# ScalarE's order of reading out a bank and splitting a weight block, in three kinds of steps

## The reference

```python
def mamba2_mixer(h, norm_w, in_w, conv_w, conv_b, ...):
    u = rms_norm(h, norm_w)
    zxbcdt = u @ in_w                       # the scan projections
    z, xbc, dt = jnp.split(zxbcdt, [D_INNER, D_INNER + CONV_CH], axis=-1)
    xbc = jax.nn.silu(conv(xbc, conv_w) + conv_b)      # causal, width 4
    ...
    y = ssd_chunked(xs, dt, a, bm, cm) + d_skip * xs   # chunks of 128 tokens
    y = y.reshape(b, s, D_INNER) * jax.nn.silu(z)
    yg = y.reshape(b, s, SSM_GROUPS, D_INNER // SSM_GROUPS)
    yg = yg * lax.rsqrt(jnp.mean(yg * yg, axis=-1, keepdims=True) + EPS)
    return (yg.reshape(b, s, D_INNER) * gnorm_w) @ out_w
# attention: q, gate = split(u @ attn_in_w); out = (swa(rope(q), k, v) * silu(gate)) @ attn_out_w
# embedding: h + act(rms_norm(h) @ ple_gate_w) * (p @ ple_proj_w)    (the p product: "embedding projection")
```

## Time and profile before

| | us |
|---|---|
| median of three runs | 1388.23 (1386.51 to 1390.5) |
| the profiled execution, its own time | 1387.61 |
| its span on the core | 1385.1 |
| TensorE busy | 1350.1 (97%) |
| VectorE busy | 831.0 (60%) |
| ScalarE busy | 677.9 (49%) |
| GpSimd busy | 525.6 (38%) |

### The profile page before, as it was taken

The page is one execution under the profiler, slowest core; times in us unless marked ns, Lnnn a source line. Parts: engine busy times, 40 slices in busy tenths (PEclk is TensorE's granted clock), DMA queues, the critical chain, the costliest instruction groups (busy, mean ns, idle before and its releaser), DMA issues.

```text
span 1385.1 us, 17824 instructions
## 1 busy us (share of the span) xinstructions
PE 1350.1 (97%) x6628; PEld 1062.1 (77%) x6628; DVE 831.0 (60%) x1417; ACT 677.9 (49%) x1130; POOL 525.6 (38%) x259
## 2 busy tenths in 40 slices
PE   9989999999999999999999999999999999999997
PEld 6867778777688878767888887766667888888886
DVE  6775554757567744785677323477755645544666
ACT  7664635636466533784565312355545332232463
POOL 3553544636220134466000344136433655555200
PEclk9999999999999999999999999999999999999999
DMA  5221222222123232211233232130012232332331
GB/s 196 94 74 47 92 70 83 77 72 77 65 97 102 77 92 93 63 44 55 99 91 122 97 135 87 37 116 16 17 46 76 94 104 91 97 101 92 122 107 61
DMA packets 33796, 116.93 MB, mean 84 GB/s; under 512 B 4140, under 2 KB 4652, under 8 KB 33456
## 3 DMA queue, kind: packets, MB, share of 16 engines
q1 hardware_dynamic: 32408, 111.62, 25.1%
q10 hardware_dynamic: 1304, 4.19, 0.8%
HBM read 113.70 MB, written 2.10 MB: 84 GB/s over the span
## 4 chain that ended last, share of the span: by engine, by line
PE 88%; DVE 5%; ACT 3%; issue 2%; DMA 1%; POOL 1%; ACTq 0%; DVEq 0%
PE bank L1306 85%; PE bank L1762 1%; PE bank L1604 1%; DMA h<-in_xT 0%; ACT wsh L864 0%; DVE arena L1957 0%; POOL arena L773 0%; DVE arena L2037 0%; PE bank L1480 0%; PE bank L1515 0%; DMA ring<-in_wstream 0%; DVE wsl L1843 0%; DVE arena L2329 0%; DVE ssacc L1838 0%; DVE arena L2243 0%
## 5 line engine op out<-in xcount | busy, mean ns | idle before, releaser
L710 POOL TENSOR_TENSOR wsl<-ring,wsh 128x1024 fp32r<-128x1024 f32 x143 | 348.8, 2440 | 543.6 <-ACT wsh L864 543.4
L864 ACT ACTIVATE wsh<-ring 128x1024 fp32r<-128x1024 f32 x196 | 207.2, 1058 | 452.8 <-PE bank L1306 429.9
L1306 PE MATMUL bank<-parts1h,wsh 128*128 128x512 f32 (+1 forms) x736 | 292.8, 398 | 6.1 <-POOL wsl L710 2.2
L1306 PE MATMUL bank<-parts1h,wsl 128*128 128x512 f32 (+1 forms) x736 | 285.6, 388 | 0.0
L1306 PE MATMUL bank<-parts1l,wsh 128*128 128x512 f32 (+1 forms) x736 | 285.6, 388 | 0.0
L1306 PE MATMUL bank<-parts0h,wsh 128*128 128x512 f32 x696 | 277.8, 399 | 3.8 <-issue 1.3
L1306 PE MATMUL bank<-parts0h,wsl 128*128 128x512 f32 x696 | 271.3, 390 | 0.0
L1306 PE MATMUL bank<-parts0l,wsh 128*128 128x512 f32 x696 | 271.1, 390 | 0.0
L1306 PEld LDWEIGHTS bank<-parts1h,wsh 128*128 128x128 f32 x736 | 138.6, 188 | 43.1 <-issue 9.7
L1306 PEld LDWEIGHTS bank<-parts0h,wsh 128*128 128x128 f32 x696 | 130.7, 188 | 40.9 <-issue 10.8
L1306 PEld LDWEIGHTS bank<-parts1l,wsh 128*128 128x128 f32 x736 | 138.8, 189 | 28.8 <-issue 2.2
(11 more groups left out here) (322 smaller groups left out, 1802.7 us busy)
## 6 DMA issues: line engine op xcount, KB each, us to landing
ring<-in_wstream SPq DMA_DIRECT2D x204, 512.0 KB, 3.5
arena<-in_alibi ACTq DMA_DIRECT2D x2, 1024.0 KB, 5.1
outT<-arena SPq DMA_DIRECT2D x8, 256.0 KB, 2.8
h<-in_xT SPq DMA_DIRECT2D x4, 256.0 KB, 6.3
h<-in_xT ACTq DMA_DIRECT2D x4, 256.0 KB, 5.8
ring<-in_wstream SPq DMA_DIRECT2D x2, 256.0 KB, 4.5
arena<-in_frow ACTq DMA_DIRECT2D x1, 512.0 KB, 3.4
arena<-in_cmpb ACTq DMA_DIRECT2D x1, 496.0 KB
```

The costliest lines, as they stand in the source:

```text
L710: return nc.gpsimd.tensor_tensor(dst, src, hi.bitcast(F32), ALU.subtract)
L864: nc.scalar.activation(wsh[n % NSET][:, :], src, ACT.Copy).then_inc(*done("high", ("high", L)))
L1306: return nc.tensor.matmul(*args, **kw)
```

## The change

ScalarE's loop over the splits of a step becomes a function, `weight_high`. For a step of the kinds proj, gate and pp it is called at the end of ScalarE's part of the step, after the readout (and, in a projection, after the opened SiLU), and not at its head; for every other kind it stays at the head. The other engines' programs are the same.

```diff
--- before.py
+++ after.py
@@ -848,20 +848,26 @@
                 k, a = step[0], step[1:]
                 if k == "ple" and a[1]:
                     square(2 * a[0] + 2 if a[0] < 2 else 7, a[1] - 1)
-                for b, n in splits_at(step):
-
-                    L = BLKNO[b]
-                    act.wait_ge(*at("loaded", L))
-                    src = ring[:, L % NSLOT, :]
-                    if n is None:
-
-                        act.wait_ge(*at("mm", *[("proj", 3, 9), ("gate", KD - 1), ("upv", FT - 1)][b[1]]))
-                        nc.scalar.activation(hnh[:, 6:8, :], src.rearrange("p (a b) -> p a b", a=2), ACT.Copy)\
-                            .then_inc(*done("high", ("high", L)))
-                    else:
-                        if n >= NSET:
-                            act.wait_ge(*at("set_free", n - NSET))
-                        nc.scalar.activation(wsh[n % NSET][:, :], src, ACT.Copy).then_inc(*done("high", ("high", L)))
+                def weight_high():
+
+                    for b, n in splits_at(step):
+
+                        L = BLKNO[b]
+                        act.wait_ge(*at("loaded", L))
+                        src = ring[:, L % NSLOT, :]
+                        if n is None:
+
+                            act.wait_ge(*at("mm", *[("proj", 3, 9), ("gate", KD - 1), ("upv", FT - 1)][b[1]]))
+                            nc.scalar.activation(hnh[:, 6:8, :], src.rearrange("p (a b) -> p a b", a=2), ACT.Copy)\
+                                .then_inc(*done("high", ("high", L)))
+                        else:
+                            if n >= NSET:
+                                act.wait_ge(*at("set_free", n - NSET))
+                            nc.scalar.activation(wsh[n % NSET][:, :], src, ACT.Copy).then_inc(*done("high", ("high", L)))
+
+                late = k in ("proj", "gate", "pp")
+                if not late:
+                    weight_high()
                 if k == "fw":
                     n, half = a
                     c = slice(SEQ * half, SEQ * half + SEQ)
@@ -1278,6 +1284,8 @@
 
                         act.wait_ge(*at("mm", "dn", m // 4 - 2, KD - 1))
                     nc.scalar.activation(xgh[:, m % 8, :], fsl[m % 2], ACT.Copy).then_inc(*done("ffhi", ("ffhi", m)))
+                if late:
+                    weight_high()
 
         @block.tensor
         def _(pe):
```

## The result

The changed kernel takes 1394.74 us (median of five runs, 1393.54 to 1395.73) against 1388.61 for the kernel before in the runs beside it: a ratio of 1.0048, 95% interval 1.0034 to 1.0062, so 4.7 to 8.6 us slower. The forecast was 1395.2. The profiled execution took 1393.54 with a span of 1391.5, 6.4 longer than before. In the experiments a difference in us is worked out from the ratio to the kernel before in the runs beside it (1.0010 is 1.4 us).

A forecast was written before the change was run, and what follows sets the result against it. TensorE, busy 1350.1 of 1385.1 us, was taken as the bound, so only its waits count. Terms 2.6 - 1.9 + 1.1 + 1.85 + 1.2 - 1.05 + 3.3, with small ones, gave +7.0: median 1395.2 us, range +4.2 to +10.

The forecast's parts named there:

- first projections, two remainders late: 40 to 76 us: TensorE waits for two remainders delayed behind readout, table load and SiLU; +2.6 us, bounds 1.5 to 3.4.
- group 0's scan, bank waits: 76 to 104 us: VectorE's taps start 0.95 us earlier, so three TensorE bank waits shrink; -1.9 us, bounds 0 to 2.6.
- end of group 1, of group 2: Before the seventh projection two readouts delay a remainder without slack; in group 2 the gating is held too: +1.1, +1.85 us.
- other small waits and collisions of the groups: Two small bank waits take off 0.3 us, smaller collisions in the last group give some 0.2 back.
- embedding projections, three places: Last embedding projections: VectorE's low halves come later, 0.4 us lost three times; +1.2 us, bounds 0 to 1.5.
- bank before the second query block: TensorE's 1.02 us wait for the bank freed by the fourth gate's readout goes; -1.05 us with the overlap.
- rotary chain and eighth gate: Three remainders hold the last rotary chain, ending at 578.5 instead of 574.38; the eighth gate starts 3.3 us late.
- Rival 3: The remainder delays the state's decay on GpSimd and TensorE feels it in four groups: +11 us, 1399; chance 0.08.
- Rival 1: Earlier taps carry everything along and the collisions don't happen: -0.4 us, near 1387.8; chance 0.26.
- Rival 2: Only the banks count, as SiLU's table load runs ahead in the first projections: -4.4 us, 1383.8; chance 0.06.
- The prediction's rule: A VectorE operation with two SBUF inputs and a GpSimd operation block each other whole; a remainder costs a chain its length.

The follow-up runs named there:

- e6: Kernel before, but in each group's first six projections ScalarE reads the bank out, then splits, then opens the SiLU: 1382.65 us, ratio 0.9958.
- e8: Changed kernel, but GpSimd's remainder at gates 5, 6 and 7 covers 256 of 1024 columns: 1389.64 us, ratio 1.0010.
- e7: Kernel before, with readout, split, SiLU in each group's first six projections, and the first four gates split late: 1381.72 us, ratio 0.9956.
- e2: Kernel before, with the split late in the eight gates alone: 1391.55 us, ratio 1.0026.
- e5: Kernel before, with the split late in the first four gates alone: 1386.37 us, ratio 0.9990.
- e9: Kernel before, with the split late in the seventh gate alone: 1385.98 us, ratio 0.9993.
- e4: Changed kernel, but four of 49 splits go first again (projections 2 and 4 of group 0, the seventh of groups 1 and 2): 1389.34 us, ratio 1.0010.
- e10: Kernel before, with the split late in the fifth and sixth gates alone: 1392.44 us, ratio 1.0042.
- e1: Kernel before, with the split late in the 35 projections alone: 1390.54 us, ratio 1.0017.
- e3: Kernel before, with the split late in the embedding projections alone: 1390.39 us, ratio 1.0011.

## Why the prediction was right, point by point

The direction was right for the reasons given: each of the places named is there, with its sign. That the total came out to 0.5 us (1395.2 against 1394.74) is partly luck: the steps that were priced came out smaller, 5.3 against 7.0, and terms that were not priced, the clock above all, brought the two profiled executions to 6.4 apart. The steps, by the balance of the two profiled executions, in us:

| step | predicted | measured |
|---|---|---|
| first projections, two remainders late | +2.6 | +1.46 +1.00 |
| group 0's scan, bank waits | -1.9 | -0.49 -0.93 -0.60 -0.46 |
| end of group 1, of group 2 | +1.1, +1.85 | +0.80, +1.51 |
| other small waits and collisions of the groups | -0.1 | 0.0 |
| embedding projections, three places | +1.2 | +0.43 +0.41 +0.41 |
| bank before the second query block | -1.05 | -1.00 |
| rotary chain and eighth gate | +3.3 | -0.88 +3.61 |
| clock behind the eighth gate | none | +2.6 |
| behind 1070 us | none | -2.0 |

**First projections.** As worked out, for the reason given: ScalarE's timeline of the changed kernel has the readout, a table load, a wait for the taps, the SiLU, and only then the split.

```profile
49.03 1.28 ACT L843 ACT_TABLE_LOAD   x1
50.73 0.63 ACT L843 ACTIVATE arena<-arena 128x512 f32<-128x512 f32 x1 [0.41 <-DVE arena L1965]
51.27 1.04 ACT L866 ACTIVATE wsh<-ring 128x1024 fp32r<-128x1024 f32 x1
```

e6 shows that the SiLU with its table load was all of it: with the split ahead of it TensorE waits for neither remainder.

**Group 0's scan.** The sum was too small by 0.6. The first wait was to gain 0.2, since the later remainder meets VectorE's preparation. It does, and holds it for 0.90 us, more than the 0.75 assumed. But the preparation itself starts 0.91 earlier, with the earlier taps in front of it, and VectorE had 0.38 of idle time before the next taps; this the prediction left out, and 0.49 was gained. In e6 the remainder comes 0.5 sooner, holds the preparation for 0.38 only, and the whole 0.92 comes. The sum also left out the wait of 0.39 at 101.29: it goes and gives 0.60, while of the 0.90 behind it only 0.46 goes.

**Ends of groups 1 and 2.** Right in place, 0.3 too high each; in group 2 the gating L2065, three operations, took 3.43 us and not 1.89, as the remainder ran until 227.0. The two readouts in front of the split cost 1.0 in both, nearly as priced. Too high was what stands ahead of them: less the balance, ScalarE's squares came 0.54 later in group 2, where 0.7 was taken, and 0.18 earlier in group 1, where nothing was taken. The tenth of a us for handovers doesn't show: in group 2 TensorE starts 0.15 us after the remainder's end, and 0.14 before.

**The groups' small terms** were the weak step. The sum of 0.0 hides four: small waits gone at the second chunk of group 1's scan (-0.77 together), then +0.72 there; +0.78 in group 2, and -0.74 behind it. The +0.72 is the mechanism of the prediction at a place where it wasn't looked for: VectorE's operation L1988, 1.21 us before (L1980 there, at 165.92), is held by a moved remainder in the changed kernel.

```profile
166.03 2.16 DVE L1988 TENSOR_TENSOR parts1h<-parts1l,con 64x1024 fp32r<-64x1024 f32 x1
...
164.72 2.40 POOL L710 TENSOR_TENSOR wsl<-ring,wsh 128x1024 fp32r<-128x1024 f32 x1 [3.56 <-ACT wsh L866]
```

The +0.78 comes of the order on GpSimd: the moved remainder, held itself to 3.37 us, stands in front of GpSimd's scan work L756 of the same step, which then holds VectorE's next operation. It came once, at 266.

```profile
263.49 3.37 POOL L710 TENSOR_TENSOR wsl<-ring,wsh 128x1024 fp32r<-128x1024 f32 x1 [3.91 <-ACT wsh L866]
266.81 1.05 POOL L756 TENSOR_TENSOR arena<-arena,cums 128x512 f32<-128x512 f32 x1
...
266.88 2.06 DVE L2030 SCALAR_TENSOR_TENSOR arena<-arena 128x1024 f32<-128x1024 f32 x1 [2.27 <-ACT arena L1021]
```

Before, that operation began at 264.36 and took 1.23; with the balance of 2.58 it begins on time (the wait for ScalarE is no loss), and takes 0.83 longer.

Rival 3's wait is there too. VectorE's sum of the states stands waiting for the decay L764 at seven places, 10.5 us together and 2.5 at most; before it was four places, 3.1 us and 0.9 at most. VectorE's timeline of the changed kernel at one of them:

```profile
105.65 0.69 DVE L2052 TENSOR_TENSOR arena<-arena,bank 128x512 f32<-128x512 f32 x1 [2.48 <-POOL arena L764]
```

But the balance doesn't rise behind any of the seven: TensorE doesn't feel it, as the prediction said against this rival.

**Gates.** The prediction asked for three operations above 2.3 us: they are 2.61, 2.63 and 2.71. It put the chain's end at 578.5; it is 580.0, less the balance of 2.12 that it came in with, 577.9. The eighth gate is 2.7 late, net, not 3.3: the wait of 0.69 for the seventh gate's readout goes (-0.88), and the wait behind the chain costs 3.61. Rival 1's condition, a chain that ends by 575.1, is what e8 brings about by the short remainder, and with it the eighth gate's wait goes. Rival 2 (only the banks count) fails in the first projections: the table load does run ahead of the wait, but the split stands behind the SiLU, and TensorE waits for the remainder. Its -4.4 lies between what the kernels get that keep the bank gains alone: by the balance -4.1 (e6) and -5.1 (e7, up to the second query block).

**What was missed** is the clock. It added 2.6 us in the changed kernel's profile. Behind 1070 us 2.0 fell away: 1.5 at 1074, where the clock fell in the kernel before and not in the changed one, and 0.5 at 1305, where kernels with no split moved after the gates (e2, e5, e9) gain 0.4 to 0.7 as well. So neither is a later stage giving time back, and the total came out right with unpriced terms against each other. This is the account of one execution of each kernel; how much of it the other executions share is not shown. The priced steps sum to 5.3 by the balance, against 7.0 predicted; group 0's scan, the ends of the groups and the eighth gate make 0.6 of the difference each.

## What to carry to other kernels

Moving an instruction to the end of its step delays everything that the step holds, also what only waits for others (here an opened SiLU and its table load); putting it behind the one instruction that mattered kept the gain and lost none of the time. Price such a move by slack, place by place: four of 49 moved splits carried 5 us, two others nearly 6, and most nothing. Here a GpSimd operation of 2.4 to 2.8 us that landed in a gapless VectorE chain cost it 2.0 to 2.2, and two of them made the chain long enough for the next one to fall inside.

## What was not expected of the hardware

**The clock falls after some waits, and not each time.** After the eighth gate's wait of 3.64 us (changed kernel, e2, e4) or 2.68 us (e10) matmuls of 0.39 us took 0.63 for a while, in all four traces; right behind the eighth gate of the eight without that wait they didn't. It took 2.6 us in the changed kernel and 1.5 to 1.6 in the other three. But the feed-forward part has a wait of 2.21 us that every kernel has alike, and there it goes both ways. Kernel before, then the changed one (TensorE):

```profile
1074.02 0.77 PE L1306 MATMUL bank<-parts1h,wsh 128*128 128x512 f32 x1 [2.21 <-POOL wsl L710]
1074.58 0.63 PE L1306 MATMUL bank<-parts1l,wsh 128*128 128x512 f32 x1
```

```profile
1082.01 0.47 PE L1314 MATMUL bank<-parts1h,wsh 128*128 128x512 f32 x1 [2.21 <-POOL wsl L710]
1082.32 0.39 PE L1314 MATMUL bank<-parts1l,wsh 128*128 128x512 f32 x1
```

The granted clock from 1065 to 1090 us was 0.93 in six of the twelve traces and 1.00 in six; it costs 1.5 us when it falls. It goes both ways at shorter waits too: behind one of 1.6 to 1.8 us for ScalarE, 11 to 14 us after the eighth gate's start, the clock fell in five of the twelve (e1, e2, e3, e5, e8; 1.2 to 1.3 us each), and behind the bank wait of 1.96 us near 81, which six traces have, in two (e3, e10; 1.6 us). What decides it at the shorter waits stays open. For a balance of two single traces it means that a us or two at such a place is no effect of an edit.

**VectorE is held in one-input operations too.** The scan's preparation L2009, a TENSOR_SCALAR of 64x512 with its input in SBUF, took 0.47 us before (L2001 there) and 1.37 in the changed kernel, where a remainder ran from 74.98 to 77.38 (in e6 0.85, where one ran until 74.09 and the operation ended at 74.37):

```profile
76.30 1.37 DVE L2009 TENSOR_SCALAR parts1l<-parts1l,con 64x512 fp32r<-64x512 f32 x1
```

The prediction's rule, drawn from operations with two inputs in SBUF, names too few. The Trainium skill (SBUF — State Buffer, Who interferes with whom) counts VectorE's two-port modes as well, besides operations with two SBUF inputs. The row agrees, with 1.37 against 0.47, if L2009 ran in such a mode, which no run here shows.
